# Moving the end of the stick gates, the memory maxima and one factor of the differential norm in a two-block transformer kernel

## The reference, cut to what matters

```python
# a layer: 6 differential heads; each output is normed over its 128 columns
w = p[:, 0] - lam * p[:, 1]
o = einsum('bhqk,bhkd->bhqd', w, v)
o = rms_norm(o, a_subln[l]) * (1.0 - lambda_init)
# b layer: 12 stick-breaking heads
a = jnp.exp(jnp.where(mask, log_beta + suffix, -jnp.inf))
# both layers: 4 memory heads over 256 memory rows
p = jax.nn.softmax(sc, axis=-1)
y = jnp.concatenate([o, om], axis=-1) * jax.nn.silu(gate)
x = x + y @ w_out
```

## Time and profile before

| | |
|---|---|
| time, median of 3 runs (lowest to highest) | 2398.34 us (2397.19 to 2399.38) |
| the profiled execution's own time | 2393.45 us |
| its span, first to last instruction | 2391.4 us |
| TensorE busy | 2234.0 us (93%) |
| mean granted TensorE clock | 0.977 of full speed |
| a layer's attention (differential and memory steps) | 196 to 325 us |
| b layer's attention (stick and memory steps) | 522 to 669 us |

### The profile page before, as it was taken

How to read it: one execution, slowest core, us unless ns; L and a number is a source line. 1 busy time by engine, 2 the same in 40 slices (tenths; PEclk the granted TensorE clock), 3 DMA queues, 4 the chain that set the end, 5 groups by cost and what they waited for, 6 DMA issues and landing times.

```text
span 2391.4 us, 27363 instructions
## 1 busy us (share of the span) xinstructions
PE 2234.0 (93%) x9994; PEld 1697.5 (71%) x9994; DVE 1165.1 (49%) x1813; ACT 930.7 (39%) x1577; POOL 1137.7 (48%) x1364
## 2 busy tenths in 40 slices
PE   6898898998898999999999999889999999999996
PEld 4676566764466666888887788666668888877885
DVE  6787866326736333024319754263330243197543
ACT  3545642345533444232223732334442322237322
POOL 3563225632144323457447575343235574575751
PEclk8999998999999999999999999999999999999998
DMA  3222112321022212233223232212122332232321
GB/s 130 71 88 71 36 53 89 97 71 36 20 78 79 62 53 93 93 97 97 88 88 106 67 110 88 79 62 62 53 88 89 97 97 89 88 106 70 108 87 62
DMA packets 52981, 191.43 MB, mean 80 GB/s; under 512 B 6000, under 2 KB 6256, under 8 KB 52336
## 3 DMA queue, kind: packets, MB, share of 16 engines
q1 hardware_dynamic: 51552, 184.44, 24.7%
q10 hardware_dynamic: 1296, 5.24, 0.6%
HBM read 187.56 MB, written 2.10 MB: 79 GB/s over the span
## 4 chain that ended last, share of the span: by engine, by line
PE 79%; DVE 8%; ACT 6%; POOL 3%; issue 3%; DMA 2%; DVEq 0%; ACTq 0%; SPq 0%
PE proj L518 20%; PE proj L520 20%; PE proj L519 20%; POOL lower L470 3%; PE score L514 3%; PE turned L514 3%; PE stat L514 2%; PE mix L514 2%; PE score L519 2%; PE score L518 2%; PE score L520 2%; PE proj L514 2%; PE ptp L739 1%; DMA raw_ring<-stream 1%; DVE small L1589 1%
## 5 line engine op out<-in xcount | busy, mean ns | idle before, releaser
L470 POOL TENSOR_TENSOR lower<-raw_ring,upper 128x256 fp32r<-128x256 f32 x1360 | 1137.5, 869 | 1210.3 <-ACT upper L1074 1209.9
L518 PE MATMUL proj<-h,upper 128*128 128x512 f32 x1496 | 609.6, 407 | 17.1 <-DVE yf L1732 7.6
L520 PE MATMUL proj<-h,lower 128*128 128x512 f32 x1496 | 586.5, 392 | 0.0
L519 PE MATMUL proj<-h,upper 128*128 128x512 f32 x1496 | 586.0, 392 | 0.0
L1074 ACT ACTIVATE upper<-raw_ring 128x1024 fp32r<-128x1024 f32 x340 | 355.8, 1057 | 560.2 <-PE proj L518 362.5
L518 PEld LDWEIGHTS proj<-h,upper 128*128 128x128 f32 x1496 | 283.8, 190 | 81.5 <-issue 11.5
L520 PEld LDWEIGHTS proj<-h,lower 128*128 128x128 f32 x1496 | 282.6, 189 | 61.1
L519 PEld LDWEIGHTS proj<-h,upper 128*128 128x128 f32 x1496 | 283.7, 190 | 56.7 <-issue 4.3
L518 PE MATMUL proj<-y,upper 128*128 128x512 f32 x628 | 254.7, 406 | 9.2 <-ACT yf L1151 3.5
L520 PE MATMUL proj<-y,lower 128*128 128x512 f32 x628 | 249.8, 398 | 0.0
L519 PE MATMUL proj<-y,upper 128*128 128x512 f32 x628 | 249.7, 398 | 0.0
(11 more groups left out here) (378 smaller groups left out, 3259.0 us busy)
## 6 DMA issues: line engine op xcount, KB each, us to landing
raw_ring<-stream SPq DMA_DIRECT2D x340, 512.0 KB, 3.5
x<-x_in SPq DMA_DIRECT2D x4, 512.0 KB, 6.9
rows<-rows_in ACTq DMA_DIRECT2D x2, 1024.0 KB, 5.3
out<-x SPq DMA_DIRECT2D x8, 256.0 KB, 2.0
memraw<-mem_in SPq DMA_DIRECT2D x1, 1024.0 KB, 11.5
memraw<-mem_in ACTq DMA_DIRECT2D x1, 1024.0 KB, 4.9
rot<-tables_in ACTq DMA_DIRECT2D x2, 512.0 KB, 3.6
ws<-ws_in ACTq DMA_DIRECT2D x2, 256.0 KB, 5.6
```

The lines of the kernel that those rows point to most:

```text
L470: ins = nc.gpsimd.tensor_tensor(lower[:, p % RING, a:b], raw_ring[:, p % RAWS, a:b], upper[:, p % RING, a:b].bitcast(FP32), ALU.subtract)
L518: first_ = nc.tensor.matmul(o, lhsT[0], rhs[0], start=start, stop=False)
L519: nc.tensor.matmul(o, lhsT[0], rhs[1], start=False, stop=False)
L520: return first_, nc.tensor.matmul(o, lhsT[1], rhs[0], start=False, stop=stop)
```

## The change

Three edits are made together.

1. In `gate_units`, stick steps get one unit each until step 39 and two in each of the steps 40 to 42. Before, steps 3, 19 and 35 had two. The total at step 44 is 48 in both. So the gates 0 to 4 are done in the steps 7, 15, 23, 31, 39 (before: 6, 14, 21, 29, 36), the last steps of their tiles.
2. VectorE makes a memory step's maxima two iterations ahead instead of three. Latent attention stays at three.
3. `root` gets an optional last step for differential tiles: ScalarE squares `std` into `yf1[:, 7, :]`, which is free at that time. `diff_finish` makes three VectorE operations instead of four: the scaling with `std` first, then `half_var` times the square, then (w + 1.5) times the scaled tile.

```diff
         if kind == "stick":
-            return min(z + 1 + (z >= 3) + (z >= 19) + (z >= 35), 8 * MT)
+            return min(z + 1 + min(max(z - 39, 0), 3), 8 * MT)
...
-        def root(S, C, scale, cols=SEQ):
+        def root(S, C, scale, cols=SEQ, square=None):
...
+            if square is not None:
+                act.wait_ge(*S.after("std", m))
+                nc.scalar.activation(square, std[:, m % 2, 0:cols], ACT.Square).then_inc(*S.mark("rooted", ("std_sq", m)))
...
-                attention(S, C, ["diff", "mem"], [(mix_square, 1, "diff"), (lambda kind, t: root(S, C, 1.0 / P), 2, "diff")],
+                attention(S, C, ["diff", "mem"], [(mix_square, 1, "diff"), (lambda kind, t: root(S, C, 1.0 / P, square=yf1[:, KT - 1, :]), 2, "diff")],
                           raw_gate, ends)
...
-                    ahead += [(maxima, 2 if kind == "diff" else 3, kind), (weights, 1, kind)]
+                    ahead += [(maxima, 3 if kind == "mla" else 2, kind), (weights, 1, kind)]
...
             def diff_finish(t, tile):
-                m, sd = inverse(S, C)
-                link(S, scaled(k1[:, t, :], mix[:, :], small[:, 13:14], sd), ("mix_used", tile), ("std_used", m))
+                m = C.next("norm")
+                w, dst = half_var[:, :], k1[:, t, :]
+                dve.wait_ge(*S.after("std", m))
+                link(S, scaled(dst, mix[:, :], small[:, 13:14], std[:, m % 2, :]), ("mix_used", tile), ("std_used", m))
+                dve.wait_ge(*S.after("std_sq", m))
+                link(S, nc.vector.tensor_tensor(w, w, yf1[:, KT - 1, :], ALU.mult))
+                link(S, nc.vector.scalar_tensor_tensor(out=dst, in0=w, scalar=1.5, in1=dst, op0=ALU.add, op1=ALU.mult),
+                     ("half_var_used", m))
```

## The result

| | us, median of the runs | lowest to highest | profiled execution | its span |
|---|---|---|---|---|
| before | 2397.77 | 2396.93 to 2399.38 (4 runs) | 2393.45 | 2391.4 |
| after | 2381.07 | 2380.38 to 2382.16 (4 runs) | 2381.15 | 2379.3 |

The ratio is 0.993, with a 95% interval of 0.9917 to 0.9943: the changed kernel is faster by 0.7%, or 16.7 us. Forecast were 2385.3 us, within 2379 to 2394. A gain of 13.0 us was summed up, and the runs have 16.7. That is more than the 9 to 16 us that the prediction gave its own forecast, and it lies at the 2380 to 2382 us of its first rival, the low clocks that go too. What of it is clock is worked out under "The clock".

A forecast was written before the change was run, and what follows sets the result against it. TensorE, busy 93% of the span, was taken as the bound, so gains come only through stalls and clock; 2.9 + 1.5 + 7.1 + 1.5 = 13.0 us off the 2398.34 us median gave 2385.3 us, range 2379 to 2394.

The forecast's parts named there:

- first rival: Low clocks at 300 to 306 and at 630 go too, 2.9 and 2.4 us more: 2380 to 2382 us; chance 0.13.
- Differential tiles 0 to 3: Differential finish on VectorE: one product fewer, square hidden under the scaling, 0.73 us at each of four places, 2.9 us.
- the rival of a late ScalarE: The Square delays exponentials and copies in ScalarE's queue; gain only 5.7 us, time 2392.6 us; chance 0.15.
- Memory steps of a: Maxima two ahead in the a layer: three TensorE waits go, 1.3 us, plus net 0.2 us; 1.5 us in all.
- Net 0.2: Two memory steps after a differential finish: the shorter finish's 0.73 is spent on later maxima, leaving 0.2 us gained.
- a new large wait of `ptp` for `pt`: Sign of being wrong: TensorE's transposes newly wait long for ScalarE's copy; no size given.
- Stick steps: Stick gates: 7.6 us of `by_gate` waits go, 1.5 clock gained, 0.8 and 1.2 paid; 7.1 us, bounds 3.5 to 8.5.
- I take 0.4: Stall for the copy of `pt` appearing anew at two stick tile boundaries, 0.2 to 0.6 us each; 0.8 in all.
- the double units' price: Double gate units moved from stalls to steps 40 to 42, one of three finding a stall; 1.2 us comes back.
- Memory steps of b: VectorE loses two idle times, 2.07 us, less 0.5 for a later copy of `pt`; 1.5 us, bounds 0 and 2.1.
- The rival that the gate wait changes its name: Transposes before the mixing wait as long for the copy; stick part gives 0 to 1, 2391.4 to 2392.4 us; chance 0.12.
- the one of a slower clock: New small stalls in stick and memory steps bring TensorE's clock down in each tile; 2409 us; chance 0.05.

The follow-up runs named there:

- the second pair: The kernel before and the changed kernel, each profiled once more without any change; 2395.25 us and a median of 2381.4 us.
- the unused square: Kernel before plus a ScalarE Square of a finished tile of `x` that nobody uses, VectorE keeping four operations; 2396.38 us in one run, 2398.12 beside it.
- the second one: Changed kernel plus one more Square in `root` right behind the first, which nobody waits for; 2384.68 us in one run.
- the square alone: Kernel before with only ScalarE's square of `std` and the three-operation finish; 2389.08 us, ratio 0.9967.
- the maxima back: Changed kernel with the memory maxima three iterations ahead again, gates and square kept; 2381.26 us, ratio 0.9933.
- the gates alone: Kernel before with only the stick gates' edit in `gate_units`; 2386.96 us, ratio 0.996.
- the maxima alone: Kernel before with only the memory maxima two iterations ahead; 2397.52 us, ratio 0.9999.
- both better versions: Changed kernel with stick units put in the stalls and memory maxima three ahead near the finishes, two behind them; 2373.14 us, ratio 0.9902.
- the three improved versions: Changed kernel with maxima three ahead near finishes, two behind (2377.42 us); with stick units in stalls, maxima three ahead (2377.63); with both ideas (2373.14).

## Why the prediction was right, point by point

**Differential tiles 0 to 3: 2.9 predicted, 3.4 measured (4.9 in the second pair, of which 1.5 is a low clock in the second execution of the kernel before).** The period of a middle tile fell from 15.37 to 14.63 us, by 0.74 for the 0.73 worked out. This is VectorE's finish in the changed kernel:

```profile
224.64 0.75 DVE L1486 SCALAR_TENSOR_TENSOR k<-mix,small,std 128x512 f32<-128x512 f32 x1
...
239.28 0.75 DVE L1486 SCALAR_TENSOR_TENSOR k<-mix,small,std 128x512 f32<-128x512 f32 x1 [0.52 <-ACT std L1121]
240.06 0.69 DVE L1731 TENSOR_TENSOR half_var<-half_var,yf 128x512 f32<-128x512 f32 x1
240.79 0.69 DVE L1732 SCALAR_TENSOR_TENSOR k<-half_var,k 128x512 f32<-128x512 f32 x1
```

and this is ScalarE beside it:

```profile
238.54 0.63 ACT L1121 ACTIVATE std<-std 128x512 f32<-128x512 f32 x1
239.21 0.63 ACT L1125 ACTIVATE yf<-std 128x512 f32<-128x512 f32 x1
...
242.69 0.47 ACT L1191 ACTIVATE prob<-turned,small 128x256 f32<-128x256 f32 x1 [1.78 <-DVE small L1595]
```

The square ends at 239.84 and the scaling that covers it at 240.03. The cover was forecast as 0.1 to 0.2 us, and the second operation follows without a wait. The stall of the last scores was to be 0.24 us. It is 0.21, and the 0.74 that it lost ahead of that stands one row block earlier:

```profile
240.68 0.92 PE L514 MATMUL score<-k,q 64*128 64x384 f32 x4 [0.74 <-ACT prob L1191]
...
243.86 0.67 PE L514 MATMUL turned<-k,q 64*128 64x512 f32 x1 [0.21 <-ACT prob L1191]
```

The 0.42 us that the sum left out came as well: the first operation of tile 0's finish took 1.11 us before and takes 0.75 now, and that tile became 1.15 us shorter. On this place the trace agrees with what the Trainium skill (SBUF — State Buffer, on the shared port pair) says. GpSimd was at work beside both first operations, from 220.52 to 222.58 us before, when the product of two SBUF tiles took 1.11, and from 222.45 to 225.21 now, when the scaling with its source in PSUM takes the same 0.75 as in the other tiles. The rule of the Trainium skill (ScalarE: Activation LUTs, Rules for kernel authors) prefers VectorE for its speed per element. Here ScalarE's square took 0.63 us and VectorE's product 0.69, so that reason does not bear on this edit. The queue, which the prediction read into the rule, isn't named there. Its cost was measured by the unused square (nothing) and by the second one (0.22 us): the rival of a late ScalarE falls for these tiles, and from a second instruction on it would begin to hold.

**Memory steps of a: 1.5 predicted, 1.65 us of stalls measured** (8.37 to 6.71; the steps took 50.5 us before and 48.8 after, 49.5 and 48.9 in the second pair). Its terms hold too. The three waits of the plain steps went, 1.33 us. "Net 0.2" for the steps beside the finishes is 0.33: the shorter finish gives 1.07 there (the square alone) and the nearer maxima take 0.74 of it back. "The stall of 2.34 us becomes about 2.1" was wrong in place but not in sum: it is 1.39, and the one before it is 1.80 for 1.10, so the two did not hide in each other and give 3.19 for 3.44. Beside the first of the two finishes it is 1.12 and 0.58 for 0.46 and 1.32. What the prediction did not see is that this price could be avoided: it wrote out that the maxima of the steps behind a finish come too late at two ahead, and the kernel that keeps three for those alone gains 1.7 us of stalls more (6.71 to 5.00). The 1.80 us, for the copy of `pt`, is also a sign that the prediction had named for being wrong, a new large wait of `ptp` for `pt`.

**Stick steps: 7.1 predicted, 8.1 in the first pair and 9.9 in the second.** These are the stretches from the start of b to the last stick mixing, 110.2 to 102.2 and 109.9 to 100.0. Both numbers hold some clock. The term is better read from the second execution of the change and the square alone, neither of which has a low clock in this stretch before the last 2.5 us: 106.5 to 100.0, which is 6.5 us for the 5.6 that the prediction had without its 1.5 us of clock. All five waits (7.6) went. "I take 0.4" for the other two boundaries was right in form; each is 0.20. The feed that was to wait at no cost waits 2.06 us on ScalarE, with nothing late behind it:

```profile
556.36 1.06 ACT L1074 ACTIVATE upper<-raw_ring 128x1024 fp32r<-128x1024 f32 x1 [2.06 <-PE proj L518]
```

The last tile, which has the double units now, grew, from 17.3 us before to 18.7, and to 18.4 in the second execution, where no low clock falls in it. Of this 0.35 us belongs to the maxima, since with the maxima back it takes 18.1, and the wait shows it, 1.46 for 1.11 with the gates alone:

```profile
618.52 0.63 PE L739 MATMUL ptp<-const,prob 128*128 128x128 f32 x4 [1.46 <-ACT pt L1209]
```

The other 0.8 us (18.1 - 17.3) is the double units' price, 1.2 in the prediction. It weighed only whether these three lie in a stall. That all units could, at 1.0 us a tile, it did not see. The low clock ahead of the fifth gate's mixing, 1.5 us, is gone in every kernel with the gate edit. But it is gone in the square alone as well, whose gates are those of before (its window at 610 to 615 has a clock of 1.00), so that it went because the stall went is not shown. The start of b, where a low clock comes and goes, gave 1.5 us in both pairs (the first mixing at 20.5 and 19.0 us, 18.6 and 17.1). What makes the second pair 1.8 us larger is mostly a low clock in the second execution of the kernel before, with a granted clock of 0.50 from 559.8 to 563.2 us: the two tiles around it took 18.29 and 18.75 us, for 17.86 and 17.56 in the first.

**Memory steps of b: 1.5 predicted, 0.9 in the first pair and 2.7 in the second.** From the last stick mixing to the end it was 36.6 us before in both executions, 35.7 after and 33.9 after again. Most of the difference between the pairs is one instruction, the last stick tile's mixing, which opens this stretch. It took 4.54 us at a low clock in both executions of the kernel before and in the first of the change, and 2.38 in the second. Before, then the change:

```profile
632.61 4.54 PE L514 MATMUL mix<-pt,v 128*64 128x512 f32 x16
```

```profile
620.51 4.54 PE L514 MATMUL mix<-pt,v 128*64 128x512 f32 x16
```

Less what this mixing took beyond 2.38 us, the stretch is 34.4 us with three ahead (before, the gates alone, the maxima back) and 33.5 with two (the maxima alone, both better versions), so the edit is worth 1.0 us here for the 1.5 forecast. The 0.5 us that the forecast paid was too small. The change has a stall that the kernel before had not:

```profile
649.51 0.41 PE L739 MATMUL ptp<-const,prob 128*128 128x128 f32 x2 [2.11 <-ACT pt L1209]
```

On ScalarE the exponential ahead of that copy waits for its maxima, which stand behind a split of VectorE:

```profile
648.52 0.47 ACT L1191 ACTIVATE prob<-turned,small 128x256 f32<-128x256 f32 x1 [2.39 <-DVE small L1595]
```

It is the same chain as in the memory steps of a, and the same sign of being wrong. The prediction also held that the low clock at 630 to 635 stays, since the steps before this mixing don't change. It stayed in the first profile of the change. In the eight profiles with the new gates the mixing took about 4.5 us once, 3.9 three times and 2.4 four times; in the five with the old gates it took 4.3 to 4.5 every time.

**The sum.** In the first pair of profiles the stages give 3.4 + 1.7 + 8.1 + 0.9 = 14.1 us for 13.0 predicted. The second pair gives 4.9 + 0.6 + 9.9 + 2.7 = 18.1 in the same stages. As the terms are read above, with the low clocks left out, they are 3.4 + 1.7 + 6.5 + 1.0 = 12.6 us, for 11.5 in the forecast without its 1.5 us of clock. Two numbers of the prediction don't come out of its terms. With all bounds the clock rival's gain is 2.9 + 3.6 + 8.5 + 2.1 + 5.3 = 22.4 us, not 19.3. And the chances count the rival of a late ScalarE as no change, a gain below 4.8 us, where its own sum gives 5.7. The rival that the gate wait changes its name has fallen by the boundary's 0.20 us, and the one of a slower clock by every run.

**The clock.** The forecast had 1.5 us of clock in its sum. Summed over the stages a, between and b of the profiles, (1 - clock) x length is 19 to 20 us in both of before, 19 and 12 in those of the change, 20 with the maxima alone, 22 with the unused square and 17 with the second one. It is 12 to 15 with the gates alone, the square alone, the maxima back, and in the three improved versions. One profile can't settle what a kernel loses. But the span and the mean clock are on record for every execution, not for the profiled ones alone. The clock is given to 0.001, which is 2.4 us here, so only means over several executions say something:

| | executions | (1 - clock) x span, mean and its standard error, us | span less that, us |
|---|---|---|---|
| before | 35 | 51.9 (0.4) | 2343.5 |
| maxima alone | 10 | 52.7 (1.0) | 2342.2 |
| square alone | 6 | 48.5 (1.0) | 2338.8 |
| gates alone | 4 | 47.1 (0.6) | 2338.2 |
| the change | 9 | 48.4 (1.1) | 2330.4 |
| both better versions | 4 | 46.8 (1.8) | 2324.5 |

The product overstates the cost where TensorE waits anyway. Still it parts the gain: of some 16.7 us about 3.5 are less time at the low clock, and 13.1 are the rest, as the terms had it. The clock's part isn't chance, since it stands in the means of kernels measured beside each other. It isn't additive either: the gates alone lose 4.8 us less than before, the square alone 3.4 less, and the change with both 3.5 less. What is missing there is of the size of the difference between the parts alone, 10.9 + 8.8 + 0.4 = 20.1 us, and together, 16.7. So the first rival came true in size, though not at its first place: the window over the memory steps of a is still low in both profiles of the change (0.56 and 0.50). Without the 2 us of clock that the forecast hadn't counted, the gain would lie inside the 9 to 16 us. Why less stall brings less low clock, and by how much, no run here shows. The loss in stage a doesn't go by the stalls: none with the square alone (7.3 us of stalls in the steps above), 3.4 with the change (6.7).

## What to carry over

Where a queue is in program order, a look-ahead is not one number: the further an operation is asked for ahead, the less it waits, and the nearer, the less stands behind it. Here three steps ahead beside a finish and two elsewhere beat either, by at least 1.7 us of stalls; the medians have 3.7, of which some is clock. Filler work of the busiest engine belongs in the steps with a known stall, and a gate's last unit right ahead of work that covers its sigmoid and product. An instruction moved to an idle engine is free only while what stands behind it in that queue has slack: the first square cost nothing, the second 0.22 us a tile.

## What the runs showed of the hardware that I had not expected

A stretch at the lower level of TensorE's clock comes back at the same places of the program, but not in every execution. It fell at 525 us in one execution of the kernel before and not in the other, and at 520 and 620 us in one of the change and not in the other, each time for some 1.7 to 2.4 us lost. Over the 13 profiles the start of b had it in nine and the memory steps of a in ten, so a place that is low once says little. The fifth stick gate had it in four of five with the old gates and in none of eight with the new.

Single executions of one kernel scatter by more than one of these edits brings: the kernel before from 2394.98 to 2400.41 us in one set of runs and from 2394.78 to 2403.59 in another. Such edits are better read from the period of a repeated tile, which agreed to 0.01 us between executions (15.37 and 15.37, 14.63 and 14.64) where no low clock fell in it.
